# Pass A's units in prompt attention dealt out among pass B's by width instead of by number

## The reference

```
s = einsum('bqhd,bkhd->bhqk', q, kf) * SCALE          # FoX: 8 heads of 64
s = s + c_q - c_k ; causal mask ; softmax ; @ v
s = einsum('bqhmd,bkhmd->bhmqk', q, kd) * SCALE       # differential: 4 heads, 2 maps of 64
s = s + T5 bias ; block-causal mask ; softmax
a = p[:, :, 0] - lam * p[:, :, 1] ; a @ v             # v of 128 columns
```

## Time and profile before

| | us |
|---|---|
| median of three runs | 2873.83 |
| profiled execution | 2870.33 |
| its span | 2868.6 |
| PE busy | 2717.3 (95%) |
| VectorE busy | 1191.1 (42%) |
| ScalarE busy | 1091.4 (38%) |
| pass B's stretch, 1426.87 to 2413.90 us | 987.03 |

### The profile page before, as it was taken

How to read it: one execution, slowest core, us unless ns; L and a number is a source line. 1 busy time by engine, 2 the same in 40 slices (tenths; PEclk the granted TensorE clock), 3 DMA queues, 4 the chain that set the end, 5 groups by cost and what they waited for, 6 DMA issues and landing times. The chain is left out here.

```text
span 2868.6 us, 37822 instructions
## 1 busy us (share of the span) xinstructions
PE 2717.3 (95%) x15257; PEld 2173.8 (76%) x15257; DVE 1191.1 (42%) x1863; ACT 1091.4 (38%) x2191; POOL 227.5 (8%) x246
## 2 busy tenths in 40 slices
PE   5999999999999999999999999999999996799998
PEld 4788888889999999999855655665565564688887
DVE  3431224325343333443333553564465352755554
ACT  3123321121222222001466666666676664422221
POOL 0100001121000000113220000000000000000000
PEclk9999999999999999999989999999999998799999
DMA  3353334458876676749250532505044102544432
GB/s 101 114 162 108 111 107 140 133 160 224 218 194 187 171 202 177 209 138 225 90 132 8 115 67 58 111 9 120 22 101 89 36 12 90 175 134 136 133 121 94
DMA packets 405774, 353.71 MB, mean 123 GB/s; under 512 B 45440, under 2 KB 368968, under 8 KB 399416
## 3 DMA queue, kind: packets, MB, share of 16 engines
q1 hardware_dynamic: 396464, 332.66, 42.8%
q0 software_dynamic: 9136, 18.63, 2.0%
HBM read 250.23 MB, written 100.71 MB: 122 GB/s over the span
## 5 line engine op out<-in xcount | busy, mean ns | idle before, releaser
L834 PE MATMUL p_acc<-p_h_hi,p_w_hi 128*128 128x384 f32 (+1 forms) x1960 | 718.9, 367 | 9.7 <-DVE p_h_lo L652 5.8
L836 PE MATMUL p_acc<-p_h_hi,p_w_lo 128*128 128x384 f32 (+1 forms) x1960 | 703.5, 359 | 0.0
L835 PE MATMUL p_acc<-p_h_lo,p_w_hi 128*128 128x384 f32 (+1 forms) x1960 | 703.1, 359 | 0.0
L1744 DVE TENSOR_REDUCE a_nmax<-a_sa 128x1 f32<-128x1024 f32 (+7 forms) x384 | 348.2, 912 | 498.9 <-PE a_sa L1821 497.9
L1724 ACT ACTIVATE a_e<-a_sb 128x512 f32<-128x512 f32 (+3 forms) x640 | 320.0, 532 | 257.7 <-PE a_sb L1847 253.5
L834 PEld LDWEIGHTS p_acc<-p_h_hi,p_w_hi 128*128 128x128 f32 x1960 | 370.4, 189 | 45.6 <-issue 10.1
L836 PEld LDWEIGHTS p_acc<-p_h_hi,p_w_lo 128*128 128x128 f32 x1960 | 370.0, 189 | 31.9
L835 PEld LDWEIGHTS p_acc<-p_h_lo,p_w_hi 128*128 128x128 f32 x1960 | 370.7, 189 | 29.9
L1695 ACT ACTIVATE a_sa<-a_sa,a_nmax 128x1024 f32<-128x1024 f32 (+7 forms) x384 | 323.3, 842 | 78.8 <-DVE a_nmax L1744 78.1
L1818 PE MATMUL a_sa<-a_k,a_q 128*128 128x512 f32 (+4 forms) x640 | 261.4, 409 | 50.1 <-ACT a_sa L1695 48.2
L1838 PE MATMUL a_sb<-a_q,a_k 128*128 128x512 f32 (+2 forms) x640 | 279.0, 436 | 2.9 <-ACT a_e L1724 2.4
(11 more groups left out here) (214 smaller groups left out, 3391.9 us busy)
## 6 DMA issues: line engine op xcount, KB each, us to landing
p_raw<-in_w_in SPq DMA_DIRECT2D x98, 512.0 KB, 5.3
s_k_raw<-in_cache_fox_k SPq DMA_DIRECT2D x32, 512.0 KB, 7.0
s_v_raw<-in_cache_fox_v SPq DMA_DIRECT2D x32, 512.0 KB, 6.3
s_k_raw<-in_cache_diff_k SPq DMA_DIRECT2D x32, 512.0 KB, 7.0
s_v_raw<-in_cache_diff_v SPq DMA_DIRECT2D x32, 512.0 KB, 6.6
a_q<-scratch_q_hi SPq DMA_DIRECT2D x32, 512.0 KB, 13.3
a_k<-scratch_k_hi SPq DMA_DIRECT2D x32, 512.0 KB, 12.0
e_pair<-scratch_gT SPq DMA_DIRECT2D x80, 192.0 KB, 2.6
```

Of the source, the lines that this page charges most:

```text
L834: nc.tensor.matmul(acc[a % 2][:, 0:n], hi, h_hi[p][:, k, at:at + n], start=(k == 0), stop=False)
L835: nc.tensor.matmul(acc[a % 2][:, 0:n], hi, h_lo[p][:, k, at:at + n], start=False, stop=False)
L836: last = nc.tensor.matmul(acc[a % 2][:, 0:n], lo, h_hi[p][:, k, at:at + n], start=False, stop=(k == DK - 1))
L1744: nc.vector.tensor_reduce(nmax[:, b % 2, c, col:col + 1], scores_of(ev[1]), axes, ALU.max, negate=True).then_inc(a_maxed, 1)
```

## The change

`target(u)` no longer counts units. Each unit has a work of its width in keys plus STEP = 300; `a_work[n]` is the work of the first n units. The lead stays 9 B units. The rate is 1.04 times the whole work over the number of B units, and `target(u)` returns the smallest number of units whose work reaches the need.

```diff
     LEAD = 9
-    RATE = 1.25
+    STEP = 300
+    a_work = list(itertools.accumulate([0] + [a_width(unit) + STEP for unit in A_UNITS]))
+    RATE = 1.04 * a_work[NA] / NU
     FINISH = ["X", 0, 1, 2, None, None, 3, 4]
...
-            return max([a_last[x] + 1 - RATE * max(0, b_first[x] - LEAD - u) for x in range(2, NB)
+            need = max([a_work[a_last[x] + 1] - RATE * max(0, b_first[x] - LEAD - u) for x in range(2, NB)
                         if b_first[x] - LEAD >= u] + [0])
+            return next(n for n in range(NA + 1) if a_work[n] >= need)
...
-            share = pass_a(min(NA, math.ceil(target(u))))
+            share = pass_a(target(u))
```

## The result

The changed kernel takes 2851.29 us (median of six runs, 2845.31 to 2853.11) where the kernel before takes 2871.87 (six runs, 2864.62 to 2879.09): ratio 0.9921, 95% interval 0.9901 to 0.9941. It is faster by some 21 us. The forecast was 2871.5 and "no change"; the range began at 2856, so the time lies outside it, 6 us beyond the 2857 of rival (a).

A forecast was written before the change was run, and what follows sets the result against it. TensorE (PE), busy 95%, bounds the kernel; terms 1.9 - 4.7 + 2 - 0.5 + 1 - 2 = -2.3 us take the profiled 2870.33 to 2868.0; the median stands 3.5 above, so 2871.5 (chance 0.36), range 2856 to 2885.

The forecast's parts named there:

- rival (a): Even rate dissolves the boundary chain: all six spells go, stops fall by a quarter; -17 us, 2857 us, chance 0.32.
- FoX and differential stops: PE waits at second units: plus 0.1 us a FoX half, plus 0.7 a differential one, 1.9 in all, bounds 12.
- F0 takes F1's place: F0 behind a 1024-key unit makes ScalarE wait; stops of 0.5 and 1.2 us at slot 2's B and A units.
- rival (c): ScalarE is held at F0 and again at F1 in each of seven boundaries; +12 us, 2884 us, chance 0.19.
- Clock: Six low-clock spells in halves two to eight; half taken as gone, minus 4.7 us, bounds 0 and minus 9.4.
- First slot: Nine units for six in the very first slot, partly hidden by low clock; plus 2 us, bounds minus 1, plus 6.
- the last half nearly unchanged: Sign that the forecast is right: the last half's length hardly moves; its stops were put at minus 0.5 us.
- Constants earlier: Pass A's results come sooner, so the last block's 0.50 us PE wait for the row's transfer goes; minus 0.5 us.
- Loads: Next pair's loads stay in slot 4; over 3 us margin even for the last map, so no effect.
- Smaller stalls: Gaps below some 0.3 us, from fewer slots delayed by F0 than by old F1; minus 2 us, bounds minus 5, plus 3.
- empty slots: Two more empty slots in a half, where B scores wait for B exponentials; plus 1 us in all.
- Rival (d): Repeating gaps mean too few buffers, so a new order only moves them and every spell stays; +2.4, 2876 us, chance 0.13.

The follow-up runs named there:

- by number: The changed kernel with STEP = 1000000, so units are dealt by count and pairs land on odd slots 3, 7, ... 39; 2819.76 us, ratio 0.9814.
- on even slots: The order by number with each pair one slot earlier, in slots 2, 6, 10, 18, ... 38; 2841.32 us, ratio 0.9884.
- filler: The kernel before with 24 small matmuls, result unused, ahead of the second unit's wait in slot 4 of every half; 2862.79 us, ratio 0.9966.

## Why the prediction was wrong

**What bounds the kernel, and why the second unit waits**: right. The PE, two `sa` buffers, the exponential behind two others on ScalarE, products as cover on odd FoX slots: the experiments by number and on even slots show just this, 6.2 us a FoX half (3.9 of it waits that the profile lists, 2.04 and 5.98 us in the third half).

**FoX and differential stops, forecast plus 1.9 us: the step that failed.** The waits on the PE fell in each FoX half from 7.9 to 5.5 us, in each differential one from 4.2 to 3.0, in the last from 3.0 to 1.3: minus 12.5 us for halves two to eight. The list of slots was right, the sizes weren't. In us a half:

| stop | forecast | measured |
|---|---|---|
| FoX, slot 0 | 1.0 | 0.76 |
| FoX, slot 2, B unit and A unit | 0.5 + 1.2 | 0.40 + 0.56 |
| FoX, narrow pairs in slots 18, 20, 22 | 0.5, 0.5, 0.7 | 0.36, 0.44, 0.31 |
| FoX, slots 31, 32, 37, 38 | 0.8, 1.2, 0.3, 1.1 | 0.27, 1.22, none, 0.76 |
| differential, slot 0 | 1.4 | 0.96 |
| differential, narrow pairs in slots 18, 20, 22 | 0.6 together | none |
| differential, the 1.15 that was to stay, and slot 38 | 1.15, 0.56 | none |
| differential, slots 29 and 35 | none, 0.2 | 0.58, 0.45 |

Each new stop was sized by the nearest old row, though the old rows were the stops that were left; the units in the same place that had not waited gave no row and weren't weighed. So nearly every guess was too long. In lengths, with the halves of before at full clock (filler), it is 126.05 to 124.0 and 119.46 to 117.77, that is 2.1 and 1.7 us a half for 2.4 and 1.2 in waits. The bounds of plus and minus 12 around plus 1.9 reached down to minus 10 only.

**F0 takes F1's place**: right in kind, and 1.0 us for 1.7. ScalarE waits 2.24 us at F0 and not at F1; rival (c) with its second wait at the logarithm is refuted, the slot-2 stops are short.

**Clock, forecast minus 4.7 us**: six spells became one, not three. By the filler's halves the six cost 9.3 us, and the one left 3.1: minus 6.2, within the bounds. That a stop brings a spell is right. The number of spells was a guess, and its reason was weak: it set 3.4 to 3.8 us of 5 with the PE busy against the 2.76 of the FoX halves, but three of the six spells, the differential ones, followed 3.39 us busy (last section), and the one that is left followed 4.04. The Trainium skill's rule ("TensorE: Matmul & The Clock Gate", section "HAM oscillation — how this bites in real kernels", penalty is throttled time times one half) gives 1.7 us for the short spells, where the halves show 1.5 to 1.6, and 3.45 for the 6.9 us of the third half, where they show 3.1. The trace agrees with the rule within 0.4 us.

**First slot, forecast plus 2**: near the sum, but by luck. The first slot grew from 13.90 to 22.05 us: its B unit starts at 1426.87 before and at 1418.84 after, and these are the starts of the next B unit, before and after:

```profile
1440.77 0.52 PE L1838 MATMUL a_sb<-a_q,a_k 128*128 128x384 f32 x1
```

```profile
1440.89 0.52 PE L1841 MATMUL a_sb<-a_q,a_k 128*128 128x384 f32 x1
```

That is 8.2 us for three units, not 6.5, and the deduction of 1.5 us for a PE that is slow anyway was wrong: the clock stayed low for longer. The first half grew by only 4.0 because its other slots became shorter, as in the other halves, which the term didn't count; the last half shrank by about 2.9 us, the three units that it no longer has. Together that is plus 1.1. The sign "the last half nearly unchanged" failed: it went from 101 to 94.3 us, with 1.7 us of stops and one spell less beside those units.

**Constants earlier, minus 0.5**: right, the DMA wait of the earlier trace rows is gone (it is counted in the last half's stops). **Loads**: right, no wait for a map in any profile; the first unit of the fourth pair starts at 1735.00, where before it started at 1745.85. **Smaller stalls, minus 2, and empty slots, plus 1**: not separable; the sum of the other terms leaves about 1 us for them.

Taken together, in the stretch: stops minus 12.5, clock minus 6.2, first half plus 4.0, three units less in the last half about minus 2.9, and by difference minus 1 for the rest, to the measured minus 18.6. **Rival (a)** had the size nearly right (minus 17) but by another reason: it said that the even rate does it. The rate is not what matters: dealing by number, at the rate of before within 0.2% but with another rounding, gains two and a half times as much. What the changed kernel gained comes for the most part from slot 4's pair, which the new order took apart (moving that pair alone gives some 16 of 21 us, 1.5 us a half of it clock). That the rest in the FoX halves comes from the pairs of slots 7, 29 and 35, which now stand on odd slots, follows from parity as other orders show it; no run takes these pairs one by one. In differential halves 29 and 35 aren't free (0.58 and 0.45 us), and why these halves gain 1.7 us at full clock is shown only as the waits that fell, 1.2 of it. **Rival (d)**: the Trainium skill ("Perfetto Trace Analysis", section "Optimization Strategy") says that a gap which keeps repeating can mean too few buffers. What the prediction drew from it, that a new order only moves the gaps, is refuted for this kernel: with the same two buffers the waits fell from 48.2 to 33.3 us in the changed kernel, and to 16.8 in the order by number. No run has a third buffer, so whether that would help is not shown.

## What to carry to other kernels

Where two streams are dealt together by a formula, look at the place in which each extra unit lands before you tune the rate: in the FoX halves of the order by number seven of nine pairs behind two products brought no stop, one slot earlier seven of nine waited 0.2 to 1.2 us in their own slot, and 1.248 in place of 1.25 had moved all nine of them. When stops are carried to a new order, size them also by the units in like places that didn't wait, and put the blocker's own chain (here ScalarE's order around F0 and F1) beside them. An idle time of 1.2 to 1.6 us on a dense PE cost nothing more here in some halves and 1.5 to 4.6 us in clock in others, and one of 2.24 us cost clock in each inner half that had it: count the spells in windows of 5 us in both profiles.

## What the runs showed of the hardware that I had not expected

Useless matmuls made the kernel faster: some 1.5 us of them in each of the eight halves, in time that was idle anyway, left none of the six spells and brought the ratio 0.9966.

The clock fell behind some short stops and not behind others like them. In the third half of the changed kernel it fell with the PE busy 4.24 and 4.04 us in the two windows of 5 us ahead of the fall. The kernel before has the same stop of 1.61 us in its fourth and its sixth half, with 3.39 us busy in the window around it; behind the one the clock fell, behind the other it didn't:

```profile
1829.80:1834.80 5.00, 3.39 (x18) 2.64 (x17) 2.61 (x7) 3.05 (x7) 0.00 (x0) 1.00 1.02 215
1834.80:1839.80 5.00, 5.00 (x21) 3.95 (x20) 3.89 (x7) 3.39 (x7) 0.08 (x1) 0.66 1.01 213
2077.00:2082.00 5.00, 3.39 (x18) 2.65 (x17) 2.73 (x6) 2.53 (x6) 0.00 (x0) 1.00 1.01 215
2082.00:2087.00 5.00, 5.00 (x27) 4.07 (x27) 3.92 (x7) 3.99 (x9) 0.00 (x0) 1.00 1.03 216
```

What makes the difference between them no run shows. And the length of a spell changes between executions of one program: the fifth half of the kernel before took 127.55 us in one profile and 129.13 in the other, with the same stops.
